# State space scan: exchanged halves of the scan-in matrices stored as a second copy and multiplied as full-width products, and the scan's loads split in two

## What is computed

```python
def s5_ssm(u, a_re, a_im, log_step, b_re, b_im, c_re, c_im, d_skip):
    uf = u.reshape(b, l, 32, 16)                      # 32 groups of 16 channels, 64 complex states each
    lam_re, lam_im = mag * cos(ang), mag * sin(ang)   # of a and step
    bb_re = coef_re * br - coef_im * bi
    bb_im = coef_re * bi + coef_im * br
    bu_re = einsum('blgc,gnc->blgn', uf, bb_re)
    bu_im = einsum('blgc,gnc->blgn', uf, bb_im)
    x_re, x_im = associative_scan(combine, (lam, bu), axis=1)
    y = einsum('blgn,gcn->blgc', x_re, c_re) - einsum('blgn,gcn->blgc', x_im, c_im)
    return y + d_skip * uf
```

## Time and profile before

| | |
|---|---|
| median of 3 runs | 2641.69 us (2641.32 to 2644.27) |
| profiled execution | 2639.71 us, span 2637.9 us |
| TensorE busy | 2582.6 us (98%) |
| VectorE busy | 1672.8 us (63%) |
| ScalarE busy | 1042.1 us (40%) |
| GpSimd busy | 343.9 us (13%) |
| mean granted TensorE clock | 0.996 of full speed |
| chain that ended last | TensorE 84%, VectorE 9%, ScalarE 4% |

### The profile page before, as it was taken

One profiled execution on the slowest core, in us unless ns is written; L12 is line 12 of the kernel. 1 busy time (PEld: TensorE's weight loads), 2 busy tenths in 40 slices (PEclk: granted clock), 3 DMA queues, 4 the chain that ended last, 5 costly groups with the idle time before them and its releaser, 6 DMA issues.

```text
span 2637.9 us, 35323 instructions
## 1 busy us (share of the span) xinstructions
PE 2582.6 (98%) x14596; PEld 2220.0 (84%) x14596; DVE 1672.8 (63%) x2605; ACT 1042.1 (40%) x1682; POOL 343.9 (13%) x361
## 2 busy tenths in 40 slices
PE   7999999999999999999999999999999999999999
PEld 7999999976688888887788788888898879888887
DVE  6854755758656544536774777647765477765765
ACT  4222233234434322235562545424454355433435
POOL 1133423020001000011000050000222014000031
PEclk9999999899999999999999999999999999999999
DMA  5243344531133233322121222332332222242322
GB/s 150 91 130 107 104 141 125 163 95 37 43 118 98 82 109 106 92 80 68 37 76 57 69 88 88 96 98 84 106 107 84 77 80 74 79 120 96 92 93 64
DMA packets 292824, 244.39 MB, mean 93 GB/s; under 512 B 19886, under 2 KB 285624, under 8 KB 292664
## 3 DMA queue, kind: packets, MB, share of 16 engines
q1 hardware_dynamic: 282599, 226.49, 27.6%
q0 software_dynamic: 5616, 13.48, 1.7%
q10 hardware_dynamic: 4448, 2.16, 0.3%
HBM read 230.80 MB, written 13.40 MB: 93 GB/s over the span
## 4 chain that ended last, share of the span: by engine, by line
PE 84%; DVE 9%; ACT 4%; issue 2%; DMA 1%; POOL 1%; SPq 0%; ACTq 0%; POOLq 0%; DVEq 0%
PE ps L578 26%; PE ps L580 26%; PE ps L579 26%; DVE ul L566 2%; ACT uh L551 1%; PE ps L2535 1%; PE ps L784 1%; PE ps L2507 1%; PE ps L1606 1%; PE ps L1852 0%; PE ps L1950 0%; DVE rbuf L799 0%; DVE tmp L2926 0%; DVE HL L2929 0%; PE ps L1917 0%
## 5 line engine op out<-in xcount | busy, mean ns | idle before, releaser
L566 DVE TENSOR_TENSOR ul<-raw,uh 128x1024 fp32r<-128x1024 f32 (+3 forms) x416 | 526.0, 1288 | 334.7 <-ACT uh L551 333.9
L578 PE MATMUL ps<-OH,uh 128*128 128x512 f32 (+1 forms) x1736 | 645.5, 372 | 4.5 <-DVE ul L566 3.8
L580 PE MATMUL ps<-OH,ul 128*128 128x512 f32 (+1 forms) x1736 | 638.6, 368 | 0.0
L579 PE MATMUL ps<-OL,uh 128*128 128x512 f32 (+1 forms) x1736 | 638.3, 368 | 0.0
L551 ACT CAST uh<-raw 128x1024 fp32r<-128x1024 f32 (+3 forms) x416 | 412.2, 1025 | 165.4 <-PE ps L580 111.1
L578 PEld LDWEIGHTS ps<-OH,uh 128*128 128x128 f32 x1736 | 327.3, 189 | 65.6 <-DVE ul L566 5.6
L579 PEld LDWEIGHTS ps<-OL,uh 128*128 128x128 f32 x1736 | 327.4, 189 | 54.7 <-issue 1.9
L580 PEld LDWEIGHTS ps<-OH,ul 128*128 128x128 f32 x1736 | 327.3, 189 | 54.7
L578 PE MATMUL ps<-HH,uh 128*128 128x512 f32 (+2 forms) x946 | 319.3, 338 | 0.6 <-DVE HL L2929 0.2
L579 PE MATMUL ps<-HL,uh 128*128 128x512 f32 (+2 forms) x946 | 317.3, 335 | 0.0
L580 PE MATMUL ps<-HH,ul 128*128 128x512 f32 (+2 forms) x946 | 317.3, 335 | 0.0
(11 more groups left out here) (457 smaller groups left out, 3702.7 us busy)
## 6 DMA issues: line engine op xcount, KB each, us to landing
raw<-in_ffn_w SPq DMA_DIRECT2D x40, 1024.0 KB, 5.2
raw<-in_ffn_w_up SPq DMA_DIRECT2D x40, 1024.0 KB, 5.0
raw<-in_ffn_w SPq DMA_DIRECT2D x32, 704.0 KB, 4.3
raw<-in_ffn_w_down SPq DMA_DIRECT2D x32, 704.0 KB, 4.3
raw<-in_w_in SPq DMA_DIRECT2D x16, 1024.0 KB, 5.4
raw<-in_gla_w_in SPq DMA_DIRECT2D x12, 1024.0 KB, 5.0
raw<-in_mla_w_o SPq DMA_DIRECT2D x8, 1024.0 KB, 4.9
raw<-in_ple_w_gate SPq DMA_DIRECT2D x8, 1024.0 KB, 5.3
```

The costliest lines, as they stand in the source:

```text
L566: e.tensor_tensor(l, src, h.bitcast(F32), SUB).then_inc(*s_wlo.up(("unit", u)))
L578: e.matmul(o, wh, xh, start=first, stop=False)
L579: e.matmul(o, wh, xl, start=False, stop=False)
L580: return e.matmul(o, wl, xh, start=False, stop=last)
```

## The change

1. While the matrices are built, the scan-in matrix is stored a second time, with the two 64-column halves of each group exchanged: two more stores per quad, in `scr_m[hq, :, 3]`.
2. A scan-in multiplies with the first copy into bank A and with the second into bank B: eight full products per quad in place of four full and eight half ones.
3. The load of three matrices is split. A first part brings both copies of the scan-in matrix, the second into a temporary tile (`MW`, in `tmps` 4 to 6); it is issued a quad ahead, and waits for the scan-in three quads back. A second part brings the two others as before, after the scan-out three quads back. TensorE waits for the first part before a scan-in, for the second before a scan-out.
4. Since `MW` lies over tiles that the norm of the mixer uses, all these loads now wait for the norm's column sums.

```diff
-        scr_m = nc.dram_tensor("scr_m", (8, 128, 3, 512), F32, kind="Internal").ap()
+        scr_m = nc.dram_tensor("scr_m", (8, 128, 4, 512), F32, kind="Internal").ap()
+        MW = [tmps[4 + i][:, 0:512] for i in range(3)]
...
                     if j == 0:
                         s_cp.wait_ge(e, ("s5t", hq))
-                        e.dma_start(scr_m[hq, :, 0, :], bgC[:, 0:512]).then_inc(*d_m0.up(("m", hq)))
+                        e.dma_start(scr_m[hq, :, 0, :], bgC[:, 0:512]).then_inc(*d_m0.up())
+                        turned, halves = (a.rearrange("p (g h n) -> p g h n", g=4, h=2)
+                                          for a in (scr_m[hq, :, 3, :], bgC[:, 0:512]))
+                        for h in range(2):
+                            e.dma_start(turned[:, :, h, :], halves[:, :, 1 - h, :]).then_inc(*d_m0.up(("m", hq)))
...
+            s_mm.wait_ge(e, ("mix", "ss", 1))
+
+            def scan_in_loads(hq):
+                if hq > 2:
+                    s_mm.wait_ge(e, ("si", hq - 3))
+                e.dma_start(MM[hq % 3][:, 0, :], scr_m[hq, :, 0, :]).then_inc(*d_mi[hq % 3].up())
+                e.dma_start(MW[hq % 3], scr_m[hq, :, 3, :]).then_inc(*d_mi[hq % 3].up(hq))
+
+            scan_in_loads(0)
             for hq in range(8):
                 i = hq % 3
+                if hq < 7:
+                    scan_in_loads(hq + 1)
                 if hq > 2:
                     s_mm.wait_ge(e, ("so", hq - 3))
-                e.dma_start(MM[i][:, :, :], scr_m[hq]).then_inc(*d_mm[i].up())
+                e.dma_start(MM[i][:, 1:3, :], scr_m[hq, :, 1:3, :]).then_inc(*d_mm[i].up())
                 e.dma_start(MT[i][:, :, :], scr_b[:, 4 * hq:4 * hq + 4, :]).then_inc(*d_mm[i].up(hq))
...
-            d_mm[hq % 3].wait_ge(e, hq)
-            for g in range(4):
-                for b, o0, n, c0 in ((bA, 0, 128, 0), (bB, 0, 64, 64), (bB, 64, 64, 0)):
-                    t = e.matmul(psum[o0:o0 + n, b, 66 * g:66 * g + 66], mm[:, 0, 128 * g + c0:128 * g + c0 + n],
-                                 UB[q][:, e0 + g, :], start=True, stop=True)
+            d_mi[hq % 3].wait_ge(e, hq)
+            for b, w in ((bA, mm[:, 0, :]), (bB, MW[hq % 3])):
+                for g in range(4):
+                    t = e.matmul(psum[:, b, 66 * g:66 * g + 66], w[:, 128 * g:128 * g + 128], UB[q][:, e0 + g, :],
+                                 start=True, stop=True)
...
             b = bk.take(e, ("so", hq))
+            d_mm[hq % 3].wait_ge(e, hq)
```

More of the change, by code:

```diff
@@ L293, in program @@
         d_kz, d_m0, d_m1, d_m2, d_k, d_b = (landing(n) for n in ("d_kz", "d_m0", "d_m1", "d_m2", "d_k", "d_b"))
-        d_mm = [landing(f"d_mm{i}") for i in range(3)]
+        d_mm, d_mi = ([landing(f"{n}{i}") for i in range(3)] for n in ("d_mm", "d_mi"))
         d_up, d_ub = ([landing(f"{n}{i}") for i in range(4)] for n in ("d_up", "d_ub"))
```

## The result

| | before | changed |
|---|---|---|
| median | 2641.69 us (7 runs, 2637.67 to 2644.27) | 2648.78 us (7 runs, 2647.85 to 2651.29) |
| ratio | | 1.0031, 95% interval 1.0021 to 1.0040 |
| profiled execution | 2639.71 us, span 2637.9 | 2649.94 us, span 2648.1 |
| mean granted clock | 0.996 | 0.994 |

A forecast was written before the change was run, and what follows sets the result against it. TensorE was taken to bound the state-space stage almost without a gap. Scan stage -8.3, GpSimd's issues +2.0 and low clock +2.5 sum to -3.8 us against the median of 2641.7: 2637.9 us, range 2633 to 2643.

The forecast's parts named there:

- Term 1: Scan-ins: eight full products replace four full and eight half; 2.48 to 1.77 us each, 5.6 us over eight quads if TensorE bounds.
- Term 2: Scan-in matrices wait only for the scan-in three quads back, so the waits of 0.78 and 0.50 us go.
- Term 3: Value products: VectorE lets the second half start only 3.0 us earlier, TensorE idles 5.3; scan stage 8.3 us earlier in all.
- Term 4: First FFN: two more GpSimd DMA issues per quad, 0.80 us each, make TensorE 2.0 us later (0.6 to about 5).
- Term 5: Matrix loads wait for the column sums, 17 us before the first scan-in; costed at nothing, u tiles the thinner cover.
- rival of a late u tile: First scan-in: u tile late behind the moved loads, wait up to 2 us, 2640; counted with the forecast's 0.46.
- a wait at the first scan-in: Sign that the prediction is wrong: TensorE waits at the first scan-in; no size given.
- the last sign of being wrong: A change of more than 2 us outside 230 to 533 us.
- Term 6: One half-clock stretch at the value products or in the run behind them, 0 to 3.4 us, taken as 2.5.
- Two low stretches: Rival: low clock at the value products and again before the last scan-out, about 2642 us; chance 0.13.
- The slower case: Rival: GpSimd's issues become the first FFN's bound; at 1.8 us per issue 5.8 us slower, 2647.5; chance 0.08.

The follow-up runs named there:

- the best kernel: The changed kernel with matrix loads early except exchanged copies, raw loads held behind the last y store, and the exchange made while loading, without extra stores: 2632.65 us, ratio 0.9965.
- the kernel with both orders: The changed kernel with quads 0 to 2's matrix loads early except the exchanged copies, and raw loads held until the last y store landed: 2637.88 us, ratio 0.9982.
- the last experiment: The best kernel plus VectorE's second value unit's low part one quad earlier and ScalarE freeing the scan-out's bank before the tables: 2634.02 us, ratio 0.9969.

## Why the prediction was wrong, point by point

**Term 1, merged products: right in size.** Scan-in 2 takes 474.47 - 472.68 = 1.79 us (predicted 1.77). By the rule of the Trainium skill (TensorE: Matmul & The Clock Gate, section LDWEIGHTS), which the prediction weighed, halves cost by their columns alone and the merge would be worth nothing. The two kernels that differ in it alone are 3.2 us apart, more than the 1.4 us that the sum credited to it.

**Term 2, loads split: right.** No scan-in or scan-out of the changed kernel waits for a matrix.

**Term 3, VectorE: right.** Predicted some 5.3 us of idle time among the value products, half behind ScalarE's copy and half behind the low part. Measured 2.79 and 1.88 us, by those two. In the best kernel, where nothing ahead of them is late, the second half starts at 496.83 us, 3.3 earlier than the 500.1 of before; predicted were 3.0.

**Term 4, GpSimd's issues: right in the total, wrong in its parts and its reach.** An issue took 0.75 us for 0.80, in quad 6:

```profile
307.08 0.58 POOL L1398 DMA_DIRECT2D scr_m<-bgC  x1 [5.04 <-ACT bgC L1451]
307.65 1.50 POOL L1402 DMA_DIRECT2D scr_m<-bgC  x2
...
310.50 1.77 POOL L1394 TENSOR_TENSOR bgA<-bgA,bgB 128x576 f32<-128x576 f32 x1
```

and TensorE waits there, where before it did not the earlier trace rows:

```profile
312.42 0.41 PE L1435 MATMUL ps<-bgA,sP 128*16 128x128 f32 x8 [0.40 <-POOL bgA L1394]
313.44 0.36 PE L579 MATMUL ps<-XH,uh 128*128 128x264 f32 x1 [0.62 <-DVE tmp L1144]
```

The column sums are 1.7 us later (predicted 2.0), but by other parts: TensorE is 0.18 us late already ahead of quad 3, quad 3 adds 0.12 where I had 1.0, and the others some 0.36 each where I had 0.25. That the total fits is in part luck. In quad 3 the slack was larger than I read it. The product starts 1.69 us later, as the issues say, but then takes 1.42 us instead of 2.31, so it ends 0.80 us later, still ahead of its use:

```profile
234.96 1.42 POOL L1394 TENSOR_TENSOR bgA<-bgA,bgB 128x576 f32<-128x576 f32 x1
...
236.53 0.41 PE L1435 MATMUL ps<-bgA,sP 128*16 128x128 f32 x8
```

Why the same product is shorter there is not shown. And the "extra traffic" that I cost at nothing left out that the same lines widen the rows of `scr_m`, and that layout costs 1.7 to 2 us by itself and more where loads are dense.

**Term 5, the loads' new start: the step that failed.** I cost it at nothing, because the matrices have 17 us. What had to be priced was not the matrices but the small u store that they now travel with. I even named the u tiles as the thinner cover, but gave them at most 2 us, without working out how much would be in flight when their store is issued. It was 3.49 us of waiting, and then some 10 us of half clock (5.2 us lost), which my rival of a late u tile did not carry. Taking the collision away gave 6.3 us. The late start by itself took the slack (0.27 us of waiting in its trace); the split loads and the wider rows, which came with it, took the rest. The prediction had "a wait at the first scan-in" among its signs of being wrong, and that sign came.

**A collision that I had not seen.** Term 3 says that TensorE catches up with VectorE. I followed this to the last scan-out ("it just doesn't bind") and stopped. What VectorE and TensorE each release behind it, raw loads and the y store, moved together: 4.1 us of wait and 2.1 of clock. Taking it away gave 4.8 us. No term and no rival has it, though the last sign of being wrong, a change of more than 2 us outside 230 to 533 us, covers it.

**Term 6, the clock: right in kind, the number of places wrong.** I took 2.5 us for one low stretch. The low clock of the changed kernel costs, from its table of stretches, 20 x 0.26 + 20 x 0.14 + 23 x 0.02 + 27 x 0.13 = 12.0 us, some of it inside idle time; before it was 6.9, from 0.83 in 470 to 490 and 0.85 in 510 to 533. Two of the three stretches stand behind the two waits that I did not have, the third behind the value products, where I expected it. That the waits bring the low clock is argued from this order in the traces, not shown: waits of 1.4 us at the Q product, before and in the kernel with both orders, leave it at 1.00 from 533 to 560, and a wait of 0.87 us in the last experiment was followed by 0.50. "Two low stretches" was my rival for the upper end, and there were three.

**The rivals.** The slower case had the wrong mechanism, GpSimd's issues as the bound; they cost 2 to 3 us. (By its own formula an issue of 1.8 us would give 6.0 us, not 5.8.) The two collisions, priced by the experiments at 6.3 and 4.8 us, are the whole miss: the kernel without them came to 2637.88, against the forecast of 2637.9. In its trace the column sums are 2.0 us later (predicted 2.0), and from there to scan-out 7 it takes 6.4 us less than before, where the sum has 8.3 less 2.5, that is 5.8. So what was in the sum was sized well. That the two medians agree to the tenth is luck: the interval is more than 2 us wide to each side, and the layout, some 2 us, was not in the sum. What the sum lacked was where the moved transfers meet others.

## What to carry to other kernels

A load that is moved meets whatever then travels. What suffered here, both times, was not the load but a small store from another queue that the next stage waits for: list what is in flight at its issue. When one engine catches up with another, list what each of them releases behind that point, since transfers that were apart may then fall together. Look also at the clock behind an idle time of TensorE among short products: here 3.5 us of wait cost 6.3 in all. And when an instruction is moved ahead in one engine's queue, look at what now stands behind it there: the copy of scan-out 0 held the tables that VectorE needed.

## What was not expected of the hardware

- Declaring a tensor with rows of 8 KB instead of 6 KB, nothing else, made loads land later: the fourth matrix's, from the tensor behind it, after 10.5 instead of 7.9 us with late, dense loads, and those from the tensor itself after 7.9 instead of 7.3. On the kernel before, where the loads are less dense, the latter stay at 4.3 us in the median and the fourth matrix's go from 5.2 to 5.8. The Trainium skill (DMA: Bandwidth & Descriptors, section Latency and other measured facts) tells of slow copies at row pitches that are large powers of two, from 512 KiB on; 8 KB is far below. Whether it is the pitch or the addresses that moved stays open: no run here parts the two, and none pads the row.
- A 264 KB store by GpSimd, 2.4 us alone, took 9.2 us beside 3.1 MB of loads. Beside 3.9 MB in larger pieces and in the old layout GpSimd waited 3.0 us less for it. How the pieces do it was not seen. The DMA engines were not busy all the while: from 442 to 444 us, with the store still under way, their share is 0.65 at 142 GB/s in the changed kernel.
- Two exchanged loads of 256-byte pieces (128 KB each, 4.3 us to landing) were no slower for the scan than one load of 256 KB of an exchanged copy.
